# Paged attention stage: keys and values of a page moved by separate transfers, in slots of their own

## The reference, cut to what matters

```python
# cache_sb_kv: (1, 640, 128, 2, 8, 64) = (layer, page, row, key or value, head, dim)
z = einsum("bqhd,bkhd->bhqk", q, k) / sqrt(64) + bias        # every key of the past and the new ones
log_1mb = where(causal, log_sigmoid(-z), 0.0)
later = cumsum(log_1mb, axis=3, reverse=True) - log_1mb      # summed from the latest key back
w = where(causal, exp(log_sigmoid(z) + later), 0.0)
out = einsum("bhqk,bkhd->bqhd", w, v)
```

## Time and profile before

| | us |
|---|---|
| median of 3 runs | 4869.67 |
| lowest and highest | 4869.15, 4869.82 |
| the profiled execution's own time | 4862.89 |
| its span | 4861.1 |
| mean granted TensorE clock over the span | 0.88 of full speed |

### The profile page before, as it was taken

The page is one execution under the profiler, slowest core; times in us unless marked ns, Lnnn a source line. Parts: engine busy times, 40 slices in busy tenths (PEclk is TensorE's granted clock), DMA queues, the critical chain, the costliest instruction groups (busy, mean ns, idle before and its releaser), DMA issues. The chain is left out here.

```text
span 4861.1 us, 65294 instructions
## 1 busy us (share of the span) xinstructions
PE 4027.5 (83%) x25189; PEld 3076.0 (63%) x25189; DVE 2138.5 (44%) x3373; ACT 1122.9 (23%) x2248; POOL 730.0 (15%) x625
## 2 busy tenths in 40 slices
PE   7978788888497699999978393945899669999995
PEld 6845566666353388989865263733446438898985
DVE  2179866666852434343451413133104343434345
ACT  1145555555300121212111211010002112111210
POOL 0034311111300210101021212120000121110102
PEclk9977799999799799999989695955896779999998
DMA  2110299999202011111110204051100201111111
GB/s 81 64 39 1 80 407 406 404 405 403 90 1 82 18 44 47 39 43 43 43 35 16 106 22 157 31 185 42 35 18 1 64 18 44 52 35 46 41 43 54
DMA packets 207051, 459.55 MB, mean 95 GB/s; under 512 B 28805, under 2 KB 113645, under 8 KB 203710
## 3 DMA queue, kind: packets, MB, share of 16 engines
q1 hardware_dynamic: 206814, 456.36, 25.7%
HBM read 440.87 MB, written 15.44 MB: 94 GB/s over the span
## 5 line engine op out<-in xcount | busy, mean ns | idle before, releaser
L1603 DVE TENSOR_TENSOR x<-x,f_d 128x512 f32<-128x512 f32 (+1 forms) x576 | 393.0, 686 | 350.5 <-PE f_d L1509 347.3
L1509 PE MATMUL f_u<-xH,f_w1h 128*128 128x364 f32 (+1 forms) x1536 | 508.3, 331 | 22.9 <-DVE f_w1l L1595 22.9
L1509 PE MATMUL f_u<-xL,f_w1h 128*128 128x364 f32 (+1 forms) x1536 | 508.1, 331 | 0.0
L1509 PE MATMUL f_u<-xH,f_w1l 128*128 128x364 f32 (+1 forms) x1536 | 507.8, 331 | 0.0
L1509 PE MATMUL f_d<-f_w2h,f_hh 128*128 128x512 f32 x1152 | 458.1, 398 | 8.8 <-DVE f_w2l L1595 8.8
L1509 PE MATMUL f_d<-f_w2h,f_hl 128*128 128x512 f32 x1152 | 457.6, 397 | 0.0
L1509 PE MATMUL f_d<-f_w2l,f_hh 128*128 128x512 f32 x1152 | 457.4, 397 | 0.0
L1582 POOL TENSOR_TENSOR f_hl<-f_h,f_hh 128x364 fp32r<-128x364 f32 (+1 forms) x192 | 184.1, 966 | 1330.0 <-ACT f_hh L1571 1330.0
L1619 DVE TENSOR_TENSOR f_h<-f_h 128x364 f32<-128x364 f32 (+1 forms) x192 | 103.1, 537 | 557.0 <-ACT f_h L1565 557.0
L1509 PEld LDWEIGHTS f_u<-xH,f_w1h 128*128 128x128 f32 x1536 | 291.7, 190 | 25.0 <-issue 23.8
L1509 PEld LDWEIGHTS f_u<-xL,f_w1h 128*128 128x128 f32 x1536 | 291.6, 190 | 1.3
(11 more groups left out here) (462 smaller groups left out, 6891.6 us busy)
## 6 DMA issues: line engine op xcount, KB each, us to landing
ss_kv<-in_cache_sb_kv SPq DMA_DIRECT2D x336, 512.0 KB, 7.9
x<-in_cache_sb_kv SPq DMA_DIRECT2D x176, 512.0 KB, 8.4
w<-in_ffn_w SPq DMA_DIRECT2D x64, 1024.0 KB, 5.5
ds_qb<-ds_q SPq DMA_DIRECT2D x24, 1024.0 KB, 6.3
ds_kc<-in_cache_dil_kv SPq DMA_DIRECT2D x16, 1024.0 KB, 7.8
x<-in_x_prompt SPq DMA_DIRECT2D x16, 512.0 KB, 6.7
pe_raw<-in_w_in_even SPq DMA_DIRECT2D x8, 1024.0 KB, 5.9
ds_kc<-in_cache_dil_kv SPq DMA_DIRECT2D x16, 512.0 KB, 6.2
```

Source lines behind the costliest of these rows:

```text
L1509: mm = pe.matmul(out, a, b, start=(n == 0), stop=(n == len(parts) - 1))
L1603: v.tensor_tensor(K.x[0:r, t, cs], K.x[0:r, t, cs], dn_b[(c * DOWN + u) % 4][0:r, :], ALU.add).then_inc(added, 1)
```

## The change

Each page's keys and values become two transfers of 256 KB. The keys of four pages of a step have a slot of their own (1 MB), and so have the values. There are `KSLOTS` = 3 slots for keys and `VSLOTS` = 4 for values. The tile `x` now holds the three key slots and the first value slot; the tile `ss_kv` shrinks to three value slots. `first_pages` loads the keys of steps 0, 1 and 2 and the values of step 0. In the stage SP's loop at g issues the keys of step g, as soon as the keys of step g - 3 have all been transposed (`k_turned`), and then the values of step g - 2 (`BEHIND` = 2), as soon as the values of step g - 6 have been used (`pv_done`). `pages` reads the page number again for the values. PE's `values` gets two waits for the landing of its values. Nothing else differs.

```diff
--- before.py
+++ after.py
@@ -541,8 +541,8 @@
 ROWS = SBH * DS
 HW = SBH * HD
 QUAD = 32
-SLOTS = 6
-LOOSE = SLOTS - 2
+KSLOTS, VSLOTS = 3, 4
+BEHIND = 2
 NSTEP = DB // 2 * STEPS
 
 
@@ -561,9 +561,10 @@
         self.bias, self.mask = sb("bias", [P, 1]), sb("mask", [P, 2, 4, NSMP])
         self.hmask, self.sel = sb("hmask", [P, 2, P]), sb("sel", [P, 4, 2 * DS])
         self.table_loaded, self.loaded, self.cleared = K.sem("si_tab"), K.sem("si_ld"), K.sem("si_clr")
-        self.kv_loaded = [[K.sem(f"si_kv{i}_{b}") for b in range(2)] for i in range(SLOTS)]
+        self.k_loaded = [[K.sem(f"si_k{i}_{b}") for b in range(2)] for i in range(KSLOTS)]
+        self.v_loaded = [[K.sem(f"si_v{i}_{b}") for b in range(2)] for i in range(VSLOTS)]
         self.cache = K.io["cache_sb_kv"][0].rearrange("n p c h d -> n p (c h d)")
-        self.kv = []
+        self.k, self.v = [], []
 
     def clear(self, v):
         v.memset(self.hmask[:, :, :], 0.0).then_inc(self.cleared, 1)
@@ -586,16 +587,18 @@
     LOADS = 8 * 5
 
     def first_pages(self, sp):
-        self.kv = [self.K.x[:, 0:4, :], self.K.x[:, 4:8, :]]
-        self.pages(sp, 0)
-        self.pages(sp, 1)
-
-    def pages(self, sp, g):
+        half = lambda t: self.K.x[:, t:t + 2, :].rearrange("p a (b n) -> p (a b) n", n=HW)
+        self.k, self.v = [half(0), half(2), half(4)], [half(6)]
+        for g in range(KSLOTS):
+            self.pages(sp, g, self.k[g], self.k_loaded[g], 0)
+        self.pages(sp, 0, self.v[0], self.v_loaded[0], HW)
+
+    def pages(self, sp, g, slot, loaded, at):
         i, s = g // STEPS, g % STEPS
         for j in range(4):
-            at = (2 * i + j // 2) * NPAGES + NPAGES - 2 - 2 * s + j % 2
-            page = sp.value_load(self.table[0:1, at:at + 1], min_val=0, max_val=self.cache.shape[0] - 1)
-            sp.dma_start(self.kv[g % SLOTS][:, j, :], self.cache[bass.ds(page, 1), :, :]).then_inc(self.kv_loaded[g % SLOTS][j // 2], 16)
+            n = (2 * i + j // 2) * NPAGES + NPAGES - 2 - 2 * s + j % 2
+            page = sp.value_load(self.table[0:1, n:n + 1], min_val=0, max_val=self.cache.shape[0] - 1)
+            sp.dma_start(slot[:, j, :], self.cache[bass.ds(page, 1), :, at:at + HW]).then_inc(loaded[j // 2], 16)
 
 
 def stick_sample(K, T, I):
@@ -604,9 +607,10 @@
     nc, io = K.nc, K.io
     with ExitStack() as ctx:
         sb = lambda name, shape, dt=F32: ctx.enter_context(nc.sbuf_tensor("ss_" + name, shape, dt))
-        more = sb("kv", [P, LOOSE, 4, 2 * HW])
-        I.kv += [more[:, i] for i in range(LOOSE)]
-        kv, kv_loaded, bias, mask, hmask, sel = I.kv, I.kv_loaded, I.bias, I.mask, I.hmask, I.sel
+        more = sb("kv", [P, VSLOTS - 1, 4, HW])
+        I.v += [more[:, i] for i in range(VSLOTS - 1)]
+        kin, vin, k_loaded, v_loaded = I.k, I.v, I.k_loaded, I.v_loaded
+        bias, mask, hmask, sel = I.bias, I.mask, I.hmask, I.sel
         kT = sb("kT", [P, 2, 4, 4, P])
         z, l, w = (sb(n, [P, 3, 2 * PAGE]) for n in ("z", "l", "w"))
         wT = sb("wT", [P, 2, 2 * PAGE])
@@ -629,10 +633,14 @@
         with nc.Block() as block:
             @block.sync
             def _(sp):
-                for g in range(2, NSTEP):
-                    if g >= SLOTS:
-                        sp.wait_ge(S["pv_done"], g - SLOTS + 1)
-                    I.pages(sp, g)
+                for g in range(KSLOTS, NSTEP + BEHIND):
+                    if g < NSTEP:
+                        sp.wait_ge(S["k_turned"], 4 * (g - KSLOTS + 1))
+                        I.pages(sp, g, kin[g % KSLOTS], k_loaded[g % KSLOTS], 0)
+                    d = g - BEHIND
+                    if d >= VSLOTS:
+                        sp.wait_ge(S["pv_done"], d - VSLOTS + 1)
+                    I.pages(sp, d, vin[d % VSLOTS], v_loaded[d % VSLOTS], HW)
 
             @block.tensor
             def _(pe):
@@ -641,9 +649,9 @@
                         if g >= 1:
                             pe.wait_ge(k_copied[j % 2], 2 * (g - 1) + j // 2 + 1)
                         if j % 2 == 0:
-                            pe.wait_ge(kv_loaded[g % SLOTS][j // 2], 32 * (g // SLOTS + 1))
+                            pe.wait_ge(k_loaded[g % KSLOTS][j // 2], 32 * (g // KSLOTS + 1))
                         for c in range(4):
-                            mm = pe.transpose(turn_b[j][:, c, :], kv[g % SLOTS][:, j, c * P:(c + 1) * P], K.ident[:, :])
+                            mm = pe.transpose(turn_b[j][:, c, :], kin[g % KSLOTS][:, j, c * P:(c + 1) * P], K.ident[:, :])
                         mm.then_inc(S["k_turned"], 1)
 
                 def scores(g):
@@ -671,6 +679,8 @@
                 def values(g):
                     s = g % STEPS
                     pe.wait_ge(S["wT_ready"], g + 1)
+                    for b in range(2):
+                        pe.wait_ge(v_loaded[g % VSLOTS][b], 32 * (g // VSLOTS + 1))
                     if s == 0 and g == 0:
                         pe.wait_ge(S["newacc"], 1)
                     elif s == 0:
@@ -680,7 +690,7 @@
                             for c in range(4):
                                 lo = QUAD * c
                                 mm = pe.matmul(ob[lo:lo + QUAD, b * P:(b + 1) * P], wT[:, g % 2, pg * P + lo:pg * P + lo + QUAD],
-                                               kv[g % SLOTS][:, 2 * b + pg, HW + c * P:HW + (c + 1) * P],
+                                               vin[g % VSLOTS][:, 2 * b + pg, c * P:(c + 1) * P],
                                                start=(s == 0 and pg == 0 and b == 0), stop=(s == END and pg == 1 and b == 1),
                                                skip_group_check=True)
                     mm.then_inc(S["pv_done"], 1)
```

## The result

The changed kernel takes 5351.5 us in the median (5347.5 to 5352.4), the kernel before on the same chip 4869.4: a ratio of **1.099**, 95% interval 1.097 to 1.101, 482 us more. The prediction was 5329 us, between 5270 and 5430. The profiled execution took 5350.94 us with a span of 5349.2.

What follows compares the result with a forecast made beforehand. SP's sequencer, at 1.117 us a transfer, was to bound the changed paged stage: 572.8 + 1125.9 + 11.4, less 0.3, plus 2.8 + 2.8 gives 1715.4, +459.4 on 1256.0; 4869.67 + 459 = 5329 us, range 5270 to 5430.

Steps and rivals of the forecast that it cites:

- SP's start in the stage: Start of SP's table reads in the paged stage, taken from the trace before as 572.8 us.
- The price of a page: SP's time per table read and transfer in the paged stage: 1.117 us, for 1008 half-page transfers 1125.9 us.
- the upper bound: One more register instruction on SP for the values' offset within the page, on 508 transfers: +46 us.
- SP's two waits: SP waiting at the stage's start for key transposes, 2.0 us at step 3 and 9.4 at step 4: 11.4 us.
- The tail: From the last issue to the stage's end: 2.8 us landing plus 2.8 us for values and gather.
- PE at half clock: Rival, paged stage: PE at 1.2 GHz bounds it at 9.4 us a step, +56 us, 5385 us; 8%.
- DMA engines as the bound: Rival, paged stage: DMA engines, not SP's time, bound it with 2048-byte packets, +33 us, 4902 us; 6%.
- Faster: Rival, last step: DMA-bound, packets' price not showing, shorter tail gains 10.4 us, 4859 us; needs under 0.65 us a transfer; 2%.
- No second read: Rival, values' issue on SP: no second table read is added, 290 us less, 5040 us; 2%.
- The DMA engines' share: Busy share of the DMA engines in the changed paged stage, forecast at about 0.61.
- PE's idle time before the key transposes: Sign in the paged stage: PE idle 4 to 5 us in a step before the key transposes.

Runs made afterwards that it cites:

- the last run: Kernel before, with keys loaded ahead of values only at steps 6, 7, 126 and 127, page numbers read once: 4863.9 us against 4868.9, ratio 0.999.
- The last experiment but one: Kernel before, with each page laid on 64 partitions, two rows on each, in packets of 8192 bytes: 5312.8 us, +444.

## Why the prediction was right

**The bound.** The step of the prediction that carried it was that SP's sequencer was 86% taken before the change and would need twice the time after. Four runs show it, each from another side: read work alone slows the kernel before by 179 us, taking reads out of the changed kernel gives back 273, two transfers from one read fall between, and handing half of the issues to POOL gives back 445. These are separate interventions on SP, and they leave no other candidate with more than the 37 us of the last one.

**The size.** The stage was forecast to end at 1715.4 and ended at 1738.6, 23.2 us later. Term by term:

- SP's start in the stage: 572.0, not 572.8: -0.8. The first issue, at 574.1, comes behind the 2.1 us of step 3's wait.
- The price of a page: 1.138 us, not 1.117, on 1008 transfers: +20.9. This is the mis-sized term. It has parts. The values' offset within the page needed no instruction more, as the upper bound had it, but lengthened the register instruction of 0.042 us. In the two stretches 1003:1007.3 (keys) and 1007.4:1011.8 (values) of the changed kernel:

```profile
L601 SPq FUSED_REGOPS  x4: 42/45/48, 1003.0 to 1006.3; - x4
```

```profile
L601 SPq FUSED_REGOPS  x4: 51/54/56, 1007.5 to 1010.8; - x4
```

  That is 3 and 12 ns, some 7 us over all. The transfer instruction took 0.350 us in the mean of the stage where it had been 0.345, another 4 us. The rest lies in the way in which 1.117 was got: the 99.1 us that were taken off as waits contain the ordinary space of about 0.05 us ahead of each of the 118 waiting reads, 6 us that belong to the price of a page. On the doubled number this is 12 us. This last share is an estimate from the usual space; together they explain the 20.9 roughly, not to the microsecond.
- SP's two waits: 2.1 and 9.6 us, where 2.0 and 9.4 were forecast: +0.3.
- The tail: 8.1 us from the last issue's end to the stage's end, where 5.3 were forecast: +2.8. About half is landing: the last transfer took 4.0 us from issue, not 2.8. The rest is the clock: from the values to the end it is 4.3 us, not 2.8. The forecast took the matmuls at full clock; they ran at half of it, 1.94 us in place of 1.08:

```profile
1734.27 1.94 PE L692 MATMUL ss_ob<-ss_kv,ss_wT 128*32 128x128 f32 x32 [3.30 <-DMA ss_kv<-in_cache_sb_kv]
...
1738.37 0.23 DVE L813 COPY xT<-ss_wb 128x64 f32<-128x64 f32 x1 [1.63 <-PE ss_wb L704]
```

The price stayed inside the bounds that the prediction gave it, -17 and +46 us.

**The rivals.** *PE at half clock*: the clock did fall, to 0.81, and moved no more than the tail; PE was busy for 5.6 of the 9.1 us of a step, and the run with kept page numbers shows it doing a step in 6.8. *DMA engines as the bound*: refuted here, by a share of 0.74. Its price, 4902, is near what the kernel before with 2048-byte pieces and the one with the values on POOL took, 4903 and 4907. *Faster*: its condition, under 0.65 us an issue, was not met; the gain at the end that it named is there, in the last run, which is 5 us shorter with both ends split. *No second read*: the profile has 1024 table reads.

**What the prediction had wrong beside the sum.** The DMA engines' share was to be 0.61 and was 0.74. That step took the engine time of a piece from a stretch with full engines and spread it over a longer time. It costs more when the engines are not full (below). PE's idle time before the key transposes was 3.3 us a step, not 4 to 5: with the clock down, PE's own work filled more of the step, 5.6 us in place of the 4.27 of the earlier trace rows.

## What to carry to other kernels

Count an issuing engine's sequencer as a resource of its own: instructions per transfer with the spaces between them, times transfers, against the time of the transfers. It shows in no busy share, and what gives it away is a total of waits that is small beside the stretch. Before a transfer is split, see how much of the issuer's time is left; if the split is wanted all the same, keep the looked-up address in a register, hand part of the issues to an idle engine, or split only where a gap at either end pays for it.

## What the runs showed of the hardware that was not expected

**A packet took more engine time where the engines were less full.** In 900 to 1200 us the changed kernel had

```profile
q1 hardware_dynamic: 37940, 69.09, 73.2%
```

which is 0.732 x 300 x 16 / 37940 = 92.6 ns for a packet in the mean, with 4213 small ones among them. The changed kernel with kept page numbers has the same transfers in closer sequence and the same share of small packets, and had 0.922 x 300 x 16 / 50167 = 88.2 ns:

```profile
q1 hardware_dynamic: 50167, 91.35, 92.2%
```

The kernel with the same pieces, two to a transfer, and full engines had 1.038 x 300 x 16 / 59355 = 83.9 ns, with a smaller share of small packets (3491). With pieces of 4096 bytes it was alike: 404 GB/s at a share of 1.02 in the kernel before, 316 at 0.90 with the table read twice. So a share of 0.74 did not mean that the rest was only a quarter: pieces of this size went at 383 GB/s elsewhere, against 232 here. What the longer time consists of was not tried.

**POOL's queue makes larger packets, to no gain.** For the same 57 MB of the same rows it used 17322 packets, and SP's queue 31275, yet both took about the same share of the engines, 50.4% and 52.4%. Fewer packets did not make the same bytes cheaper.

**The price of a transfer instruction went by its shape, not its bytes.** 128 rows of 4096 and 128 rows of 2048 bytes cost 0.338 us each; 128 rows in two pieces cost 0.543, with the same bytes as the first. The last experiment but one, with 64 partitions and two rows on each, had 0.468:

```profile
L599 SPq DMA_DIRECT2D ss_kv<-in_cache_sb_kv x336: 468/469/1037, 576.8 to 1657.3; - x168
```
